# Two-layer hybrid step: value products with held values and streamed pairs of heads, and scores of both differential maps issued side by side

## What is computed

```python
def window_attention(q, k, v, kc, vc, sink):       # latent tokens; context tokens: own keys and sink only
    ...
    p = jax.nn.softmax(jnp.concatenate([s_lat, s_ctx, s_sink], axis=-1), axis=-1)
    ...
    o = jnp.einsum('bngrqk,bnkgd->bnqgrd', p_lat, vn) + jnp.einsum('bngrqm,bmgd->bnqgrd', p_ctx, vc)
def diff_attention(q, k, v, lam):
    ...
        s = jnp.einsum('bqhcd,bkhcd->bhcqk', qb, k).astype(jnp.float32) * scale
        p = jax.nn.softmax(s, axis=-1)
        a = p[:, :, 0] - lam * p[:, :, 1]
        return jnp.einsum('bhqk,bkhe->bqhe', a.astype(v.dtype), v)
# in trunk_layer:
    o_diff = (rmsnorm(o_diff, p['g_diff']) * (1.0 - lam_init)).reshape(b, l, DIFF_H * DIFF_DV)
def mla_attention(q, k_nope, k_rope, v):
    ...
        p = jax.nn.softmax(s.astype(jnp.float32) * scale, axis=-1)
        return jnp.einsum('bhqk,bkhe->bqhe', p.astype(v.dtype), v)
# then
    branches = jnp.einsum('blnc,ncd->blnd', branches, p['w_branch'])
    gates = jax.nn.sigmoid((h @ p['w_gate'] + p['b_gate']).reshape(b, l, N_BRANCH, D_MODEL))
    mixed = jnp.sum(gates * branches, axis=2) @ p['w_out']
    x = x + gate1 * mixed
```

## Time and profile before

| | us |
|---|---|
| median of 3 runs | 2593.49 (2593.43 to 2594.24) |
| profiled execution, own time | 2593.88 |
| its span | 2592.1 |
| PE busy | 2472.2 (95%) |
| DVE busy | 1162.7 (45%) |
| ACT busy | 883.4 (34%) |
| POOL busy | 753.2 (29%) |

### The profile page before, as it was taken

How to read it: one execution, slowest core, us unless ns; L and a number is a source line. 1 busy time by engine, 2 the same in 40 slices (tenths; PEclk the granted TensorE clock), 3 DMA queues, 4 the chain that set the end, 5 groups by cost and what they waited for, 6 DMA issues and landing times.

```text
span 2592.1 us, 41615 instructions
## 1 busy us (share of the span) xinstructions
PE 2472.2 (95%) x16003; PEld 2248.1 (87%) x16003; DVE 1162.7 (45%) x2006; ACT 883.4 (34%) x1488; POOL 753.2 (29%) x519
## 2 busy tenths in 40 slices
PE   5999999999998999999979999999999989999998
PEld 3887787878898999999958877877789989999998
DVE  3233336532235762663732333365223357627446
ACT  3424334443223441332243332445332143313221
POOL 1311131011132544444323202211012325535442
PEclk7989999999999999999979899999999989999999
DMA  7412222122322222221172122322223212222211
GB/s 267 137 37 68 87 76 74 52 82 82 103 85 66 66 82 77 71 82 58 47 264 73 46 78 71 96 66 64 78 82 102 82 54 67 81 75 73 82 61 54
DMA packets 234468, 216.85 MB, mean 84 GB/s; under 512 B 8590, under 2 KB 217878, under 8 KB 234006
## 3 DMA queue, kind: packets, MB, share of 16 engines
q1 hardware_dynamic: 226614, 193.99, 23.7%
q10 hardware_dynamic: 7648, 20.09, 2.3%
HBM read 204.98 MB, written 9.08 MB: 83 GB/s over the span
## 4 chain that ended last, share of the span: by engine, by line
issue 70%; POOL 29%; PE 1%; DVE 0%; POOLq 0%; DVEq 0%; ACT 0%
POOL w_lo L640 29%; PE ps L684 1%; POOLq L637 0%; DVE y_tm L1934 0%; PE ps L1158 0%; PE ps L1151 0%; DVEq L232 0%; DVE x L1856 0%; DVE ss L1850 0%; DVE sq L1848 0%; ACT st L1494 0%; POOLq L632 0%; POOL token L631 0%; POOLq L640 0%; DVEq L1904 0%
## 5 line engine op out<-in xcount | busy, mean ns | idle before, releaser
L640 POOL TENSOR_TENSOR w_lo<-raw,w_hi 128x512 fp32r<-128x512 f32 (+1 forms) x512 | 752.8, 1502 | 1805.1 <-ACT w_hi L1185 1805.1
L684 PE MATMUL ps<-h_hi,w_hi 128*128 128x320 f32 x2432 | 633.2, 316 | 20.4 <-DVE gprod L1589 8.2
L684 PE MATMUL ps<-h_lo,w_hi 128*128 128x320 f32 x2432 | 620.6, 311 | 0.0
L684 PE MATMUL ps<-h_hi,w_lo 128*128 128x320 f32 x2432 | 620.3, 311 | 0.0
L684 PEld LDWEIGHTS ps<-h_hi,w_hi 128*128 128x128 f32 x2432 | 427.1, 190 | 31.9 <-DVE h_lo L1560 8.4
L684 PEld LDWEIGHTS ps<-h_lo,w_hi 128*128 128x128 f32 x2432 | 426.6, 190 | 0.2
L684 PEld LDWEIGHTS ps<-h_hi,w_lo 128*128 128x128 f32 x2432 | 426.3, 189 | 0.0
L1185 ACT ACTIVATE w_hi<-raw 128x2048 fp32r<-128x2048 f32 (+2 forms) x132 | 245.7, 1861 | 339.9 <-PE ps L684 241.5
L1613 DVE TENSOR_REDUCE stat<-ps 128x1 f32<-128x640 f32 (+3 forms) x160 | 108.4, 677 | 281.7 <-PE ps L804 256.6
L740 PE MATMUL ps<-w_hi,h_hi 128*128 128x512 f32 (+1 forms) x480 | 182.7, 381 | 13.3 <-DVE h_lo L1560 12.2
L740 PE MATMUL ps<-w_lo,h_hi 128*128 128x512 f32 (+1 forms) x480 | 181.4, 378 | 0.0
(11 more groups left out here) (254 smaller groups left out, 3304.3 us busy)
## 6 DMA issues: line engine op xcount, KB each, us to landing
raw<-in_w_mod SPq DMA_DIRECT2D x48, 1024.0 KB, 6.2
raw<-in_w_up SPq DMA_DIRECT2D x88, 512.0 KB, 4.6
raw<-in_w_gate SPq DMA_DIRECT2D x32, 1024.0 KB, 5.5
raw<-in_w_in SPq DMA_DIRECT2D x20, 1024.0 KB, 5.2
raw<-in_w_down SPq DMA_DIRECT2D x16, 1024.0 KB, 5.0
w_br<-in_w_branch ACTq DMA_DIRECT2D x8, 1024.0 KB, 6.1
raw<-in_w_out SPq DMA_DIRECT2D x8, 1024.0 KB, 5.1
raw<-in_w_down SPq DMA_DIRECT2D x8, 768.0 KB, 4.7
```

The costliest lines, as they stand in the source:

```text
L640: ins = nc.gpsimd.tensor_tensor(w_lo[s % WS][:, c0:c1], raw[u % RAW][:, c0:c1], w_hi[s % WS][:, c0:c1].bitcast(F32), ALU.subtract)
L684: ins = mm(out, w_at(w_hl[wi]), at_(x_hl[xi]), start=first and q == 0, stop=final and q == 2)
```

## The change

1. **Value products.** The weights are now the values of one key block and head (64 columns), and the transposed probabilities stream (128 columns). Heads go in pairs, the even one to partitions 0 to 63 of bank 6, the odd one to 64 to 127, so that the output stands transposed. A pair is issued at even steps only. ACT (take_heads) copies four heads' output straight to o_t, which is double now; for br 2 it also squares it. o_transposes(1), (3) and the transposes of the diff output in the MLA stage are gone.
2. **Normalisation before the product.** DVE divides a head's probabilities by their sum (probs_normed), for br 2 with the combination of the maps in it, one head behind the scores and ahead of the next head's mask and maximum.
3. **LAG = 2.** Transposes are those of head i-2, the pair's product that of heads i-4 and i-3; STEPS = 4T + 4. Buffers of probabilities: six maps for br 2, and four transposed ones.
4. **Scores of diff.** Runs of both maps alternate, behind one wait for both maps of the head before.
5. **RMS norm of diff.** Sums of squares over 64 channels by products with ones on PE in two slots of the MLA stage, Sqrt on ACT, reciprocal and one multiply on DVE; g_diff is a column of vcol.
6. **The layer loop** is a Python loop over two layers, so that the program is written out twice, with constants in the waits.

```diff
-        STEPS = 4 * T + 3
+        LAG = 2
+        STEPS = 4 * T + LAG + 2
...
         @block.tensor
-            with pe.Fori(0, DEPTH) as li:
+            for li in range(DEPTH):
...
-                        if i < 4 * T and br > 1:
+                        if i < 4 * T and br == 2:
                             a_ = head0 + i
                             _, t, h = HEADS[a_]
-                            for m2 in range(2 if br == 2 else 1):
-                                m = FIRST_MAP[a_] + m2
-                                pe.wait_ge(exp_done.sem, now(exp_done, m - 1))
-                                b = 2 * (m % 2)
-                                for col, k0, n in score_runs(key_blocks(br, t)):
-                                    last = mm(bank(b, col, col + n), query(br, t, h, m2), keys(br, h, m2, k0, n),
+                            pe.wait_ge(exp_done.sem, now(exp_done, FIRST_MAP[a_]))
+                            runs = score_runs(key_blocks(br, t))
+                            for col, k0, n in runs:
+                                for m2 in range(2):
+                                    last = mm(bank(2 * m2, col, col + n), query(br, t, h, m2), keys(br, h, m2, k0, n),
                                               start=True, stop=True)
...
-                        if 1 <= i <= 4 * T:
-                            a_ = head0 + i - 1
+                        if LAG <= i < 4 * T + LAG:
+                            a_ = head0 + i - LAG
                             m = FIRST_MAP[a_]
-                            if br == 2:
-                                pe.wait_ge(comb_done.sem, now(comb_done, i))
-                            else:
-                                pe.wait_ge(exp_done.sem, now(exp_done, m + 1))
+                            pe.wait_ge(norm_done.sem, now(norm_done, a_ + 1))
...
-                        if 2 <= i <= 4 * T + 1:
-                            a_ = head0 + i - 2
+                        if LAG + 1 <= i <= 4 * T + LAG and (i - LAG) % 2 == 0:
+                            a_ = head0 + i - LAG - 2
                             _, t, h = HEADS[a_]
-                            pe.wait_ge(pt_done.sem, now(pt_done, a_ + 1))
+                            pe.wait_ge(pt_done.sem, now(pt_done, a_ + 2))
                             if h == 0 and a_:
                                 pe.wait_ge(oev_done.sem, now(oev_done, T * (br - 1) + t))
                             kb = key_blocks(br, t)
                             for j, b in enumerate(kb):
-                                last = mm(bank(6, 64 * h, 64 * h + 64), probs_t[:, a_ % 2, j, :], values(br, b, h),
-                                          start=j == 0, stop=j == len(kb) - 1)
+                                for odd in range(2):
+                                    last = mm(ps[64 * odd:64 * odd + 64, 6 * BANK + 64 * h:6 * BANK + 64 * h + P], values(br, b, h + odd),
+                                              turned(a_ + odd)[:, j, :], start=j == 0, stop=j == len(kb) - 1)
                             last.then_inc(pv_mm.sem, 1)
...
+                for c2 in range(2):
+                    b = slot()
+                    for q in range(2):
+                        for odd in range(2):
+                            rows_ = slice(64 * odd, 64 * odd + 64)
+                            last = mm(ps[rows_, (b + q) * BANK:(b + q) * BANK + HALF], ones[rows_, 0:64], o_sq[rows_, c2, q * HALF:(q + 1) * HALF],
+                                      start=True, stop=True)
+                    last.then_inc(mla_mm.sem, 1)
...
+                def take_heads(br, t):
+
+                    sc.wait_ge(pv_mm.sem, now(pv_mm, 2 * (T * (br - 1) + t + 1)))
+                    src = bank(6, 0, BW).rearrange("p (k n) -> p k n", k=2)
+                    if br == 2:
+                        act_(o_sq[:, :, t * P:(t + 1) * P], src, ACT.Square)
+                    act_(o_t[br % 2][:, :, t * P:(t + 1) * P], src, ACT.Copy).then_inc(oev_done.sem, 1)
...
+                    def probs_normed(a_):
...
+                        ve.wait_ge(exp_done.sem, now(exp_done, m + maps))
+                        if br == 1:
+                            tt(stat[:, 5, c0:c0 + 1], den, stat[:, 3, c0:c0 + 1], ALU.add).then_inc(vstep.sem, 1)
...
+                        V.reciprocal(rec, den).then_inc(vstep.sem, 1)
...
+                        if br == 2:
...
+                            ts(p2, p2, stat[:, 4, c0 + 1:c0 + 2], lam[:], ALU.mult, ALU.mult).then_inc(vstep.sem, 1)
...
+                            stt(p, p, stat[:, 4, c0:c0 + 1], p2, ALU.mult, ALU.add).then_inc(norm_done.sem, 1)
+                        else:
+                            ts(p, p, rec, None, ALU.mult).then_inc(norm_done.sem, 1)
+
                     for i in range(STEPS):
...
+                        if 1 <= i <= 4 * T:
+                            probs_normed(head0 + i - 1)
                         if i < 4 * T:
                             for m2 in range(2 if br == 2 else 1):
                                 softmax_bias(head0 + i, m2)
```

226 lines of the change are left out of this document (103 added, 123 removed).

## The result

The changed kernel takes 2605.55 us (median of 6 runs, 2602.14 to 2607.86) against 2594.72 us before (6 runs, 2593.43 to 2597.34). The ratio is 1.0041 (95% interval 1.0031 to 1.0052): **slower by 0.4%**, 11 us, where 3 us less had been forecast. The time lies in the range of the prediction, its sign is wrong. Its profiled execution has a span of 2603.5 us, 11.4 more than before.

A forecast was written before the change was run, and what follows sets the result against it. TensorE, busy 2472 of 2592 us, was taken as the bound. From 2593.9: 2 x 3 off for the loops, 2 x 1.8 for transposes and RMS norm, 8 added for pairs, 5 off for layer loop, 4 added for clock: 2591; range 2565 to 2625.

The forecast's parts named there:

- A: All loops: waits for bank 7 take back what the value products save; 2591 us, bounds 2576 to 2608; chance 0.60.
- C: Modulation row's steps: TensorE's clock falls after 1.25 us idle, 2611 to 2635 us; chance 0.21.
- D: Value products: column halves don't overlap, each pair takes 2 x 1.08 us, 2650 us in all; chance 0.05.
- the signs of being wrong: Gate chunks starting well before 3.9 us after the scores, or a window chain longer by a microsecond or two.
- Waits for bank 7 take back the odd steps' saving: Odd steps: fill items wait uncovered; saved 0.15 or 0 us a diff step, 0.35 or 0.6 an MLA step.
- The longest stall of the diff loop goes, -0.9: Diff loop: the 2.05 us wait for the combined maps goes, about half moves to the fill item; -0.9 us a layer.
- A pair costs 0.15 more than a head: Even steps: a pair's value product takes 1.3 us against one head's 1.15; +8 us in all, bounds 0 to +12.
- Window attention +0.1 a layer, bounds -3 to +4: Window loop: normalisation in the chain between heads, plus a longer ending, nets +0.1 us a layer.
- MLA stage +0.6: MLA stage: ten transposes go, 16 ones-product records come, one wait less, one square root more; +0.6 us a layer.
- Transposes of the window output, -1.2: After window attention: the ten output transposes go, saving 1.2 us a layer.
- Layer loop -5: Between layers: the unrolled loop loses its branch and instruction refill; -5 us, bounds -6 and -1.
- Clock +4: Longer loop endings, two a layer: one or two further stretches at half clock in all, +4 us.

The follow-up runs named there:

- e5: Kernel before, value product of each odd head cut to its first key block (the rest left out of the output): 2578.06 us, ratio 0.9935.
- e6: Changed kernel, a pair's value product split in two pieces, one in the even and one in the odd step: 2595.08 us, ratio 0.9993.
- e1: Kernel before with only its layer loop written out twice: 2583.09 us, ratio 0.9949.
- e3: Changed kernel without sum, reciprocal and multiply of the window normalisation (output not normalised): 2590.97 us, ratio 0.9989.
- e2: Changed kernel, window normalisation of a head moved behind the next head's mask and maximum on VectorE: 2610.57 us, ratio 1.0061.
- e9: Changed kernel, window normalisation moved behind mask, maximum and first fill read, ahead of the second read on VectorE: 2595.38 us, ratio 1.0010.
- e4: Changed kernel, rotary step of the MLA queries put between the two halves of the diff normalisation on VectorE: 2600.17 us, ratio 1.0020.
- e11: Kernel before with only its layer loop written out, run again on one chip with a four-edit kernel: 2581.28 us, ratio 0.9949.

## Why the prediction was wrong

The mechanism of A, the forecast (waits for bank 7), held. The sign failed at two steps that the prediction priced at about nothing: the normalisation in the window attention, and the two reciprocals in the MLA stage. "Slower" had a chance of 0.40, but 0.26 of it stood on C and D, neither of which came. Of the signs of being wrong that it named, the second came: a window chain longer by more than a microsecond or two.

- **Waits for bank 7 take back the odd steps' saving**: right, and e5 and e6 show it apart. Branch then gate in diff: 0.19 won (forecast 0.15), but this nearness is luck. The gate stood 4.00 us after the scores (469.85 to 473.85), not 4.12, which was read ahead of a modulation; and it now stands 3.79 after them, not 3.99, as VectorE's read starts 0.12 earlier in written-out code. In the looped kernel e5 the same step saves 0.07. Row then gate in diff: 0.15 (0); e1 has the same 7.15 us with its value product in the step, so the product's part is 0, as forecast. MLA: 0.21 and 0.68 (0.35 and 0.6).
- **The longest stall of the diff loop goes, -0.9**: it didn't go. In place of 2.05 us for the combined maps TensorE waits 2.93 for the row's read in the same step (463.06). From scores to scores the step takes 10.5 us, 8.8 at equal clock, against 9.1 in e1: 0.3 won.
- **A pair costs 0.15 more than a head**: too small by half. From branch to gate it is 0.31 (2.42 against 2.11), before a modulation row 0.18. The term was mis-sized at its other end: the head's 1.15 us was read where a row of 32-column groups follows (480.51 to 481.66), and before a gate it is 1.03 (492.93 to 493.96). So the head pays for a change of arrangement there (0.12) and not before a gate, while the pair takes 1.24 to 1.25 before either. The pair itself, forecast at 1.30, measured 1.34: 0.09 for the entry and 1.25.
- **Window attention +0.1 a layer, bounds -3 to +4**: this step failed. It is +5.4 and +6.5 against before and +7.0 and +8.1 against e1, outside the bounds. The working put prices on the chain of a head (mask, exponents, multiply) and none on the fill reads that stand behind it on VectorE, nor on operations that took longer beside GpSimd's (1.19 to 1.27 us in place of 0.42 and 0.49, in 4 of the 32 multiplies of the latent tiles). e3 shows the size, 8.3 to 8.9 us, of which 4.6 and 5.4 at equal clock; e2 and e9 show that the place in VectorE's order decides on about half of it.
- **MLA stage +0.6, "multiplies lie beside TensorE's work"**: this failed too. The step took the normalisation for two multiplies and passed over their reciprocals, of 4.15 us each; nothing in the trace of before has a reciprocal wider than 20 columns, and it was not bounded. With the loop's end it is +4.8 and +7.8 (+4.8 and +4.4 at equal clock), where +2.1 stood in the sum. e4 shows 2.1 to 2.5 of it as the wait behind the reciprocals.
- **Transposes of the window output, -1.2**: nothing of it shows. At equal clock in_product 3 to 5 takes 76.4 to 76.5 us before, 76.2 in e1 and 76.2 to 76.3 after, and a gate chunk waits 1.24 us for GpSimd's w_lo at 385.23, where before the transposes stood and it waited for nothing. It is again work that covered a wait.
- **Layer loop -5**: its boundary gave -6.3, right. Steps and clock gave as much again (e1), -12.8 in all. Register arithmetic was taken at 0 with a bound of -2 a layer; it was 1.8 at equal clock, although the prediction saw nothing of it in VectorE's timelines.
- **Scores side by side: 0**: right. The steps start 8 records and their transposes 1.28 us apart as before (504.22 to 505.50).
- **Clock +4**: in the whole it was less, +2 (160 us at half clock in place of 157, mean clock 0.969 in both), but it moved between stages by more than that. After, layer 0 has stretches at half clock at the end of the window attention, behind the 2.93 us wait at 463, and in the MLA stage. Rival C didn't happen: but for the step at 463, rows' steps wait 1.05 us, not 1.25, and take 7.15 us, less than before; one of them is followed by a drop (520.5, layer 0).
- **The sum**, in lengths of stages of both layers against the kernel before, with the forecast in brackets (its 8 us for pairs shared evenly among the three loops): window attention +11.9 (+2.9), end of diff with MLA stage +12.6 (+4.2), in_product 3 to 5 +0.6 (-2.4), diff loop -4.2 (-0.6), MLA attention -5.7 (-5.5), change of layers -6.3 (-5), all else +3 (0), clock in the lengths (+4). That is +12 against -2.4, the 14 us between 2591 and 2605.5; 17 us lie in the first two entries, and some of them were made good by others.

## What to carry over

An in-order engine's new work is priced by what stands behind it in its queue, at each of its places: list the next three reads behind it and who waits for each, and try the place between two reads. Time an operation's kind by a row of its own width before calling it covered; a reciprocal isn't a multiply. Where small work covers a wait, taking it out saves only what exceeds the wait, so spread it rather than gather it; and test the plain half of a mixed change alone, since here the written-out loop was worth 13 us and hid that the rest cost 24. Compare stages of two profiles at equal clock before giving their difference a cause.

## What the runs showed of the hardware

- A reciprocal over 128x640 on VectorE took 4.15 us, where a multiply with two tensor inputs of that size took 0.89 beside it.
- Two products of 64 weight columns in the two column halves ran together: 20 records of 128 streamed columns in 1.25 us, 12 in 0.81. Between full-array products the halves cost 0.09 us at their start and about 0.15 once within (an estimate from the two counts).
- Between the layers TensorE was idle for 7.62 us on the hardware loop and for 1.30 in written-out code. Steps were shorter in written-out code too, with 3.25 us in place of 3.37 from scores to the read of the branch product.
- On VectorE a sum over 128x1 took 1.15 us and a multiply over 128x512 1.26 us beside GpSimd's subtractions (e2), 0.15 and 0.49 without.
- The same step with a wait of 2.05 us ahead was followed by 6.7 us at a clock of 0.50 before, with 1.96 by none in e1, and with 1.96 and 1.98 by 3.4 us in e11, which is the same kernel as e1. The end of diff with the MLA stage had drops in some kernels and not in others. A forecast of a few us has this as its floor.
